# Another start address modulo 512 bytes for TensorE's operands in one decoder block

## The reference

```python
mod = (silu(c) @ w_ada + b_ada)                         # six vectors of 2048
h = rmsnorm(x, g_pre_mix) * (1 + scale_m) + shift_m
z = h @ w_in                                            # 2048 x 12112, then split
y_a = mla_branch(q_lat, kv_lat, k_rope, ...) @ w_branch_a    # 8 heads
y_b = gla_branch(gq, gk, gv, g_lr, g_og, ...) @ w_branch_b   # 4 heads
merged = sigmoid(gate_a) * y_a + sigmoid(gate_b) * y_b
x = x + gate_m * rmsnorm(merged @ w_mix_out, g_post_mix)
h = rmsnorm(x, g_pre_ffn) * (1 + scale_f) + shift_f
u = h @ w_ffn_up                                        # 2048 x 11264
a, val = split(causal_conv3(u))
f = (gelu(a) * val) @ w_ffn_down                        # 5632 x 2048
out = x + gate_f * rmsnorm(f, g_post_ffn)
```

## Time and profile before

| | |
|---|---|
| median of three runs | 1612.02 us (1609.37 to 1613.06) |
| the profiled execution's own time | 1611.82 us |
| its span | 1610.0 us |
| TensorE busy, share of the span | 99% |
| weight loads, share of the span | 93% |
| VectorE, ScalarE busy | 70%, 51% |
| mean granted TensorE clock | 0.995 |
| mean DMA rate | 242 GB/s |

### The profile page before, as it was taken

How to read it: one execution, slowest core, us unless ns; L and a number is a source line. 1 busy time by engine, 2 the same in 40 slices (tenths; PEclk the granted TensorE clock), 3 DMA queues, 4 the chain that set the end, 5 groups by cost and what they waited for, 6 DMA issues and landing times.

```text
span 1610.0 us, 29554 instructions
## 1 busy us (share of the span) xinstructions
PE 1590.1 (99%) x11788; PEld 1496.4 (93%) x11788; DVE 1134.1 (70%) x1331; ACT 818.7 (51%) x1068; POOL 7.3 (0%) x11
## 2 busy tenths in 40 slices
PE   7999999999999999999999999999999999999998
PEld 7999999879999999999888999999999999888886
DVE  5888767886977786877766677777777665644444
ACT  5567776656544643434446545455554544434332
POOL 0000000001000000000000000000000000000000
PEclk9999999999999999999999999999999999999999
DMA  9999988873458887877864777777777656555553
GB/s 370 355 326 345 324 268 256 284 251 128 128 195 293 284 293 242 290 268 261 325 225 129 242 238 236 236 246 236 252 236 221 200 184 209 185 196 194 184 195 143
DMA packets 190648, 389.41 MB, mean 242 GB/s; under 512 B 18386, under 2 KB 31058, under 8 KB 189794
## 3 DMA queue, kind: packets, MB, share of 16 engines
q1 hardware_dynamic: 185666, 370.33, 68.8%
q10 hardware_dynamic: 4898, 17.90, 3.3%
HBM read 386.09 MB, written 2.10 MB: 241 GB/s over the span
## 4 chain that ended last, share of the span: by engine, by line
PE 94%; DVE 3%; ACT 2%; issue 1%; DMA 0%; DVEq 0%; ACTq 0%
PE ps L579 20%; PE ps L581 20%; PE ps L583 20%; PE ps L606 8%; PE ps L608 8%; PE ps L607 8%; PE ps L783 2%; PE ps L531 1%; DVE w_lo L1385 1%; PE ps L722 1%; DMA x_tok<-in_x 0%; PE ps L690 0%; PE ps L798 0%; PE ps L721 0%; PE ps L656 0%
## 5 line engine op out<-in xcount | busy, mean ns | idle before, releaser
L1385 DVE TENSOR_TENSOR w_lo<-raw,w_hi 128x1024 fp32r<-128x1024 f32 x530 | 625.7, 1221 | 422.4 <-ACT w_hi L969 421.6
L969 ACT ACTIVATE w_hi<-raw 128x1024 fp32r<-128x1024 f32 x530 | 533.0, 1052 | 654.5 <-PE ps L583 426.4
L579 PE MATMUL ps<-h2t,w_hi 128*128 128x256 f32 x1408 | 389.8, 277 | 0.6 <-DVE h2t L1815 0.6
L581 PE MATMUL ps<-h2t,w_hi 128*128 128x256 f32 x1408 | 388.7, 276 | 0.0
L583 PE MATMUL ps<-h2t,w_lo 128*128 128x256 f32 x1408 | 388.7, 276 | 0.0
L579 PE MATMUL ps<-ht,w_hi 128*128 128x256 f32 x1104 | 310.5, 281 | 0.0
L581 PE MATMUL ps<-ht,w_hi 128*128 128x256 f32 x1104 | 306.8, 278 | 0.0
L583 PE MATMUL ps<-ht,w_lo 128*128 128x256 f32 x1104 | 306.7, 278 | 0.0
L579 PEld LDWEIGHTS ps<-h2t,w_hi 128*128 128x128 f32 x1408 | 264.3, 188 | 0.8 <-issue 0.8
L581 PEld LDWEIGHTS ps<-h2t,w_hi 128*128 128x128 f32 x1408 | 264.4, 188 | 0.0
L583 PEld LDWEIGHTS ps<-h2t,w_lo 128*128 128x128 f32 x1408 | 264.3, 188 | 0.0
(11 more groups left out here) (279 smaller groups left out, 2032.8 us busy)
## 6 DMA issues: line engine op xcount, KB each, us to landing
raw<-in_w_ffn_up SPq DMA_DIRECT2D x176, 512.0 KB, 4.5
raw<-in_w_in SPq DMA_DIRECT2D x168, 512.0 KB, 5.2
ada<-in_w_ada SPq DMA_DIRECT2D x148, 512.0 KB, 6.5
raw<-in_w_ffn_down SPq DMA_DIRECT2D x88, 512.0 KB, 4.0
raw<-in_w_branch_b SPq DMA_DIRECT2D x32, 512.0 KB, 5.4
raw<-in_w_mix_out SPq DMA_DIRECT2D x32, 512.0 KB, 5.0
ada<-in_w_ada ACTq DMA_DIRECT2D x32, 512.0 KB, 4.1
raw<-in_w_branch_a SPq DMA_DIRECT2D x16, 512.0 KB, 5.3
```

The source lines that it names most:

```text
L579: mm(o, w_hi[:, s, k, cols], moving[:, kt, 0], start=opens, stop=False, skip_group_check=True)
L581: mm(o, w_hi[:, s, k, cols], moving[:, kt, 1], start=False, stop=False, skip_group_check=True)
L969: A(w_hi[:, slot], raw[:, slot], ACT.Copy).then_inc(hi_done, 1)
L1385: V.tensor_tensor(w_lo[:, slot], raw[:, slot], w_hi[:, slot].bitcast(F32), ALU.subtract)\
```

## The change

`at` adds a number of bytes to the filler: for five buffers one of their own from a table, and for all others 512 where they lie 48 KB or more into the shared region, which leaves their place modulo 512 as it was and makes room.

```diff
+OFFSET = {"ht": 192, "h2t": 448, "og_s": 320, "ot": 384, "hid": 832}
...
-            with nc.sbuf_tensor(name + "_before", [P, max(kb, 0) * 256 + 8], F32):
+            begin = max(kb, 0) * 1024 + 32 + OFFSET.get(name, 512 if kb >= 48 else 0)
+            with nc.sbuf_tensor(name + "_before", [P, begin // 4], F32):
```

## The result

The changed kernel takes 1653.76 us (1653.61 to 1654.14), the kernel before beside it 1611.87 us: a ratio of 1.0262, with a 95% interval of 1.0245 to 1.028. It is slower by 42 us, and the forecast of 1597.0 us as well as the range up to 1632 us were wrong.

What follows compares the result with a forecast made beforehand. TensorE was taken to bound the kernel through matmul start-to-start distance; -14.8 us (narrow) + 0 (wide) + 0 (writes) against 1611.8 us gave 1597.0 us, with an 8-in-10 range of 1578 to 1632 us.

Steps and rivals of the forecast that it cites:

- What bounds the kernel: Whole kernel: TensorE busy 99% of the span, so time is the number of matmuls by their start-to-start distance.
- The term of the narrow matmuls: 8688 256-column matmuls on h2t, ht, og_s, ot: from 113.3 to 111.6 ns each, 14.8 us less.
- the floor of 110.0: Lowest narrow distance, read from weight loads of the transposes at L933: 3.3 ns less each, 28.7 us.
- the better of two already seen: Narrow matmuls on ht after restarts: 118 ns, or 114 ns with a pace between; today's rhythm is the faster.
- the upper bound, 118 ns: Highest narrow distance, from the slow rhythm behind a restart: 4.7 ns more each, 40.8 us over 8688.
- The term of the wide matmuls: 1440 512-column matmuls holding hid or ht: taken as 0, between 22.5 us less and 6.8 us more.
- The terms at nothing: VectorE and ScalarE writes into moved buffers, at most 1.0 us and hidden; DMA writes unchanged; faster TensorE still fed.
- No effect: Rival, whole kernel: start address does not matter, distances stay 113.3 and 228.9 ns, 1611.8 us within 3; chance 0.28.
- The slower rival: FFN up falls into a 118 ns rhythm, 19.9 us more, 1632 us; all four buffers 1653 us; chance 0.25.
- the last tenth: Slow end of the whole-kernel forecast: a chance of 0.1 for times above 1632 us, outside the 8-in-10 range.
- The signs named beforehand: Profile, L579 to L583: under 113 ns in two stages if forecast holds, unchanged if no effect, 118 in FFN up if slower.
- the control: Wide matmuls on merged and passes on lat_s, left at 320 modulo 512; merged was to stay at 229 ns.

Runs made afterwards that it cites:

- the map: Four runs giving stages of the kernel before other separations between moving and stationary operand starts, lat_s left in place: 1647.23, 1661.71, 1670.51 and 1647.84 us.

## Why the prediction was wrong

**What bounds the kernel** was right: the time is the number of matmuls by their distance, no other engine entered, and the difference of 42.3 us is all in distances. That addresses change the distance was right too. That they could give some of it back was not, for narrow matmuls: at none of seventeen separations did they settle under 113.3 ns, and the wide ones gained 2.2 of the 15.6 ns named as stall.

**The term of the narrow matmuls** is the step that failed. It took -1.7 ns for each of 8688, half of the way to the floor of 110.0. Measured: +5.3 (h2t), +5.3 (ht), +6.5 (og_s) and +4.2 (ot); by the lengths of the stages the term came out at about +43 us instead of -14.8. Half of the way was taken because of four places one might come free of its stall; none did. The reason given, that today's rhythm "is the better of two already seen, which a shift need not lose since the `pace` matmuls stay", was the wrong reading of the earlier trace rows. That there were two rhythms at the same addresses, one of them better, said that the kernel stood in a good state that could be lost. The `pace` matmuls stayed, and the good rhythm went all the same: in the map 113.4 ns exists at one separation only. The floor of 110.0 ns was reached at no place. It was read from transposes of plain float32, and no run shows that it is the price of a weight load. The Trainium skill, "TensorE: Matmul & The Clock Gate", section "Wait — 56ns, not 53.3ns?", gives 109.2 and 215.8 ns by its N / 2.4 + about 2.5 ns; no place reached these either, the best being 113.3 and 226.7. And the upper bound, 118 ns, was too low for og_s at 119.9 and for h2t and ht at 118.7, since it was taken from slow stretches at the separation of 192, not from the new ones.

**The term of the wide matmuls** was taken at nothing, because the held block is read for a fourth of the bytes. Measured: -2.2 ns on hid, 1056 matmuls, 2.3 us; +3.5 ns on ht, 384 matmuls, 1.3 us. The size of a read is no measure of what its place costs.

**The terms at nothing** held: writes of VectorE and ScalarE (busy 1134.2 and 818.8 us against 1134.1 and 818.7), DMA, the feeding of TensorE.

**The rivals.** No effect was excluded by the stages of the changed kernel: with no semaphore unmet, the same matmuls on og_s take 113.4 ns at one separation of the two operands and 119.9 ns at another. The Trainium skill, "SBUF — State Buffer", section "Who interferes with whom", says that TensorE never waits on anyone. The traces disagree with it as far as TensorE's own two operands go. The slower rival had the right sign, place and nearly the price (19.9 us for FFN up, measured 22.1), and the text even gave the 1653 us for all four buffers. That this is the measured time is in part luck: the true distances lie from 0.3 ns under 118 to 1.9 over it, and the two wide terms that it leaves out nearly cancel. The rival got a chance of 0.25, with all four at once put in the last tenth. It had them as independent, since four buffers got four places; but a separation that is the one good value among seventeen makes all four wrong together. It also took the rhythm of 118 ns for one that lasts "for a few tens of matmuls", where the kernel before has up to 142 in a row. Nor has every pass on ht, h2t, og_s and ot the same distance within a nanosecond, as the rival of no effect had it. The mechanism of the slower rival was half right: not the same rhythm of 118 ns that a restart shows, but rhythms of their own at every other separation.

**The signs named beforehand** worked: the control did not move, and it was the stages one by one that told place from layout.

## What to carry to other kernels

Where TensorE's distance from start to start is above columns divided by clock with no semaphore unmet, the separation of the two operands' starts, modulo 256 bytes, is a knob: for this stream of a 128 x 128 weight load and a 256-column fp32r matmul it moves the distance by up to 7%, for 512 columns by 3%. Before such a layout is changed, for whatever reason, note the separation of each stage, and try one stage at a time; a pad in front of an earlier buffer that shifts only one of the two operands can cost about 3% of the whole kernel (1612 to 1655 and 1662 us here), and neither the waits nor the busy shares show it. Several stages with several places make one run a map, if one stage is left as the control.

## What the runs showed of the hardware

- The distance between matmuls that each load new weights depends on where the moving and the stationary operand begin in memory, one against the other. The separation counts, not either place: weights and activations both 64 bytes on give 113.4 ns again, the weights alone 118.7.
- It repeats after 256 bytes as far as four pairs of separations go, which agree within 0.1 ns, and it is sharp: 113.4 ns at 192, 121.7 at 196, 119.2 at 176 and 208.
- 512-column matmuls have other best separations, 0 and 240, at 226.7 ns; the worst read 233.4. None of the eleven tried reached the 213.3 ns that the prediction works out for the stream alone.
- The starts follow each other in fixed rhythms, among them periods of one (og_s in the changed kernel, 120 ns each), three (the kernel before) and five (h2t in the changed kernel). The same separation can hold more than one, 113.4 and 118 ns at 192. Why a given separation has its rhythm was not found; that the reads of the two operands meet in the same part of the memory is a guess, and no run here shows it.
